# mLSTM products with queries on partitions and a ones column, head norm summed along rows, attention transposes one slot later

## What is computed

```python
num = einsum('bhcjs,bhcsd->bhcjd', P, v) + inter_w[..., None] * einsum('bhcde,bhcje->bhcjd', C_prev, q)
den = sum(P, axis=-1) + inter_w * einsum('bhce,bhcje->bhcj', n_prev, q)
h = num / maximum(abs(den), exp(-m_j))[..., None]
...
h = h_fw + h_bw
h = h * rsqrt(mean(h * h, axis=-1, keepdims=True) + EPS) * norm_g
y = sigmoid(o_pre) * h
```

## Time and profile before

| | us |
|---|---|
| median of 3 runs | 2229.85 (2228.08 to 2233.18) |
| the profiled execution, its own time | 2229.88 |
| its span, first to last instruction | 2228.1 |
| mean granted TensorE clock | 0.988 |
| first slot of cross attention to the first merge unit | 63.2 to 429.8 |

### The profile page before, as it was taken

The page is one execution under the profiler, slowest core; times in us unless marked ns, Lnnn a source line. Parts: engine busy times, 40 slices in busy tenths (PEclk is TensorE's granted clock), DMA queues, the critical chain, the costliest instruction groups (busy, mean ns, idle before and its releaser), DMA issues.

```text
span 2228.1 us, 29871 instructions
## 1 busy us (share of the span) xinstructions
PE 2153.9 (97%) x9840; PEld 1733.5 (78%) x9840; DVE 1019.4 (46%) x1694; ACT 864.7 (39%) x1252; POOL 1203.1 (54%) x1601
## 2 busy tenths in 40 slices
PE   6989999799999999999999999999999989999999
PEld 5867666588888888888878888887777767888887
DVE  5466587633345544223444555213655545554400
ACT  5334323443343443332134443324455445344321
POOL 7533322677755556655455556656444426655653
PEclk9989999899999999999999999999999999999999
DMA  6213411133333233333322323332322203223332
GB/s 217 89 48 109 114 49 38 48 99 104 109 95 94 94 96 103 95 93 95 104 88 93 104 94 93 96 102 68 116 90 71 86 29 103 95 94 104 91 102 72
DMA packets 61480, 205.06 MB, mean 92 GB/s; under 512 B 6848, under 2 KB 6976, under 8 KB 61392
## 3 DMA queue, kind: packets, MB, share of 16 engines
q1 hardware_dynamic: 61200, 203.65, 29.6%
q10 hardware_dynamic: 192, 0.30, 0.1%
HBM read 201.52 MB, written 2.39 MB: 92 GB/s over the span
## 4 chain that ended last, share of the span: by engine, by line
PE 87%; DVE 6%; ACT 2%; POOL 2%; DVEq 1%; issue 1%; DMA 1%; ACTq 0%; SPq 0%
PE bank L1424 27%; PE bank L1426 26%; PE bank L1425 26%; POOL WL L425 1%; PE bank L1632 1%; PE bank L1658 1%; PE bank L1644 1%; PE bank L1695 1%; PE bank L1697 1%; PE bank L1696 1%; PE bank L1465 1%; PE bank L1676 1%; DMA RAW<-in_w_att 0%; POOL YL L476 0%; PE bank L1561 0%
## 5 line engine op out<-in xcount | busy, mean ns | idle before, releaser
L425 POOL TENSOR_TENSOR WL<-RAW,WH 128x256 fp32r<-128x256 f32 x1496 | 1157.2, 807 | 967.7 <-ACT WH L537 967.3
L1424 PE MATMUL bank<-XH,WH 128*128 128x512 f32 x1840 | 728.5, 396 | 2.9 <-DVE XQ L896 2.0
L1426 PE MATMUL bank<-XH,WL 128*128 128x512 f32 x1840 | 717.1, 390 | 0.0
L1425 PE MATMUL bank<-XL,WH 128*128 128x512 f32 x1840 | 716.9, 390 | 0.0
L537 ACT ACTIVATE WH<-RAW 128x1024 fp32r<-128x1024 f32 x374 | 392.1, 1051 | 250.1 <-PE bank L1426 224.7
L1424 PEld LDWEIGHTS bank<-XH,WH 128*128 128x128 f32 x1840 | 345.9, 188 | 86.6 <-issue 5.4
L1425 PEld LDWEIGHTS bank<-XL,WH 128*128 128x128 f32 x1840 | 346.0, 188 | 73.7 <-issue 3.1
L1426 PEld LDWEIGHTS bank<-XH,WL 128*128 128x128 f32 x1840 | 345.8, 188 | 72.9
L1424 PE MATMUL bank<-FH,WH 128*128 128x512 f32 x528 | 205.4, 389 | 0.0
L1425 PE MATMUL bank<-FL,WH 128*128 128x512 f32 x528 | 205.4, 389 | 0.0
L1426 PE MATMUL bank<-FH,WL 128*128 128x512 f32 x528 | 205.4, 389 | 0.0
(11 more groups left out here) (277 smaller groups left out, 2441.6 us busy)
## 6 DMA issues: line engine op xcount, KB each, us to landing
RAW<-in_w_up SPq DMA_DIRECT2D x132, 512.0 KB, 3.5
RAW<-in_w_att SPq DMA_DIRECT2D x47, 512.0 KB, 3.6
RAW<-in_w_down SPq DMA_DIRECT2D x48, 448.0 KB, 3.3
RAW<-in_w_fa SPq DMA_DIRECT2D x32, 512.0 KB, 3.5
RAW<-in_w_down SPq DMA_DIRECT2D x24, 512.0 KB, 3.5
RAW<-in_w_ain SPq DMA_DIRECT2D x24, 512.0 KB, 3.5
RAW<-in_w_mrg SPq DMA_DIRECT2D x18, 512.0 KB, 3.6
RAW<-in_w_mrg SPq DMA_DIRECT2D x22, 256.0 KB, 2.7
```

What stands on the lines that cost most here:

```text
L425: last = nc.gpsimd.tensor_tensor(WL[:, s, w], RAW[:, s, w], WH[:, s, w].bitcast(F32), ALU.subtract)
L1424: mm(dst[:, 0:width], WH[:, s, w], a, start=start and k == 0, stop=False)
L1425: mm(dst[:, 0:width], WH[:, s, w], b, start=False, stop=False)
L1426: last = mm(dst[:, 0:width], WL[:, s, w], a, start=False, stop=stop and k == kc - 1)
```

## The change

1. mLSTM products: the decayed scores of a block of 128 queries are now the weights and the values the moving operand, `V` with a 129th column of ones beside it. A product gives numerator and denominator, queries on partitions. Five products of 129 columns a step take the place of four of up to 512. They fill three banks (`HBANK`).
2. The denominators are now 8 columns for a head; thresholds come transposed (`THR`, a new extra `thr`, four small transposes). `head_out` scales and adds in 128-column pieces. The norm is a row sum on ACT (`Square` with a sum), its scale is applied on ACT, and PE then turns the head back (`ht`, four transposes, one slot before where `hn` stood).
3. The exponents move from DVE to ACT (`Relu` with a bias, before `Exp`), with two buffers in turn. `UE` holds two rows a head instead of four: 6 row loads after the wait instead of 12, and one write of gates instead of two.
4. Attention: transposes of step g - 1 come in slot g and its products in slot g + 1, scaling likewise one slot later; buffers are halved in turn. The last attention slot transposes two steps.
5. The gain of the norm is applied where `YH` and `YL` of the mLSTM are formed.

```diff
+def lagging(st, lag):
+    if st and st in SIDX:
+        g = SIDX[st]
+        return tuple(STEPS[n] for n in (range(g - lag, g - lag + 1) if st != LAST_STEP else range(g - lag, g + 1))
+                     if n >= 0)
+    return ()
...
-    _ex = [("hn", _st[1] - 1)] if 3 in finishing(_st) else []
+    _ex = [("ht", _st[1] - 1)] if 2 in finishing(_st) else []
...
+    if _t == GATE_T + 5:
+        _ex.append(("tr", "thr", 0))
...
-                    for g in range(2):
-                        for d in range(2):
-                            row = gates_d[g, 32 * d + h, :]
-                            sp.dma_start(UE[:, UE_AT[h], 2 * g + d, :], row.partition_broadcast(P)).then_inc(ue_in, 16)
+                    for d in range(2):
+                        row = gates_d[0, 32 * d + h, :]
+                        sp.dma_start(UE[:, h, d, :], row.partition_broadcast(P)).then_inc(ue_in, 16)
...
             if st and st[0] == "ml":
-                act.wait_ge(e_arg, m + 1)
-                A_(SX[:, 0, P * s:S], SX[:, 0, P * s:S], ACT.Exp, scale=-1.0)
-                A_(SX[:, 1, 0:P * (s + 1)], SX[:, 1, 0:P * (s + 1)], ACT.Exp, scale=-1.0).then_inc(e_ready, 1)
...
+                    act.wait_ge(ms_read, m - 1)
+                for d in range(2):
+                    w = slice(P * s, S) if d == 0 else slice(0, P * (s + 1))
+                    A_(SXM[m % 2][:, d, w], UE[:, h, d, w], ACT.Relu, bias=UT[:, s, 32 * d + h:32 * d + h + 1])
+                act.drain()
+                for d in range(2):
+                    w = slice(P * s, S) if d == 0 else slice(0, P * (s + 1))
+                    e = SXM[m % 2][:, d, w]
+                    last = A_(e, e, ACT.Exp, scale=-1.0)
+                last.then_inc(e_ready, 1)
...
-                if 2 in finishing(st):
-                    act.wait_ge(h_ready, h + 1)
-                    A_(SQ[:], FI[:, 0, :], ACT.Square).then_inc(h_sq, 1)
+            if 1 in finishing(st):
+                act.preload_act_table_set(LN_EXP)
+                act.wait_ge(h_ready, h + 1)
+                for q in range(TB):
+                    A_(SQ[:, q * P:(q + 1) * P], HQ[:, q, :], ACT.Square, accum_out=HS[:, q:q + 1])
...
+                A_(HS[:], HS[:], ACT.Ln, scale=1.0 / P, bias=EPSC[:, 0:1])
...
+                A_(HS[:], HS[:], ACT.Exp, scale=-0.5)
...
+                for q in range(TB):
+                    last = A_(HQ[:, q, :], HQ[:, q, :], ACT.Copy, scale=HS[:, q:q + 1])
+                last.then_inc(h_rs, 1)
...
+        def head_out(h):
+            dve.wait_ge(mpv_done, 4 * h + 4)
+            for n, sl in ((0, slice(0, 3)), (1, slice(3, 6)), (2, slice(6, 8))):
+                den = HBANK[n][:, :, P]
+                thr = THR[:, 0:3, 32 * n + h] if n < 2 else THR[:, 3, h:64:32]
+                v.scalar_tensor_tensor(out=ND[:, sl], in0=den, scalar=-1.0, in1=thr, op0=ALU.mult, op1=ALU.max)
...
+            v.reciprocal(ND[:], ND[:])
+            for q in range(TB):
...
+                v.tensor_scalar(HQ[:, q, :], HBANK[b][:, n, 0:P], ND[:, c:c + 1], None, ALU.mult)
+            for q in range(TB):
...
+                last = v.scalar_tensor_tensor(out=HQ[:, q, :], in0=HBANK[b][:, n, 0:P], scalar=ND[:, c:c + 1],
+                                              in1=HQ[:, q, :], op0=ALU.mult, op1=ALU.add)
+            last.then_inc(nd_free, 1)
...
-            mm(bank[4][:, P * s:S], V[:, h % 2, s, :], fw, start=s == 0, stop=s == 3)
-            mm(bank[5][:, P * s:S], ONES[:], fw, start=s == 0, stop=s == 3)
-            mm(bank[6][:, 0:w], V[:, h % 2, s, :], bw, start=s == 0, stop=s == 3)
-            mm(bank[7][:, 0:w], ONES[:], bw, start=s == 0, stop=s == 3).then_inc(mpv_done, 1)
+            for d in range(2):
+                for q in range(s, TB) if d == 0 else range(s + 1):
+                    b, n = h_place(d, q)
+                    last = mm(HBANK[b][:, n, :], (PT, PB)[d][:, m % 2, P * q:P * (q + 1)], V[:, h % 2, s, :],
+                              start=first, stop=final)
+            last.then_inc(mpv_done, 1)
...
-            if before and before[0] in ("xa", "na"):
-                products(before)
+            for ts in lagging(st, 2):
+                if ts not in STEPS[-2:]:
+                    products(ts)
...
-            if st and st[0] in ("xa", "na"):
+            for ts in lagging(st, 1):
+                g = SIDX[ts]
                 for j in range(2):
                     pe.wait_ge(p_ready, 2 * g + j + 1)
```

More of the change, by code:

```diff
@@ L81, in finishing @@
         return ()
[L82 removed]
+    return (st[2],) if st[0] == "ml" else ((0, 1), (2,), (), ())[st[2]]
 UNITS = [u for u, _ in SLOTS if u is not None]
@@ L109 @@
             VEV[_e[1:]] = len(VEV)
-            if _e[1] != "nav64":
+            if _e[1] not in ("nav64", "thr"):
                 VSRC[_e[1:]] = len(VSRC)
@@ L292, in col, with turn_of, half_of, h_place @@
         return PAR[rows, bass.ds(COL[name] + n, 1)]
+    def turn_of(g, j):
+        return slice(2 * (g % 2) + j, 2 * (g % 2) + j + 1)
+    def half_of(t, g, j):
+        return t[:, j, M * (g % 2):M * (g % 2) + M]
+    HBANK = [bank[4][:, 0:3 * (P + 1)].rearrange("p (q e) -> p q e", e=P + 1),
+             bank[5][:, 0:3 * (P + 1)].rearrange("p (q e) -> p q e", e=P + 1),
+             bank[6][:, 0:2 * (P + 1)].rearrange("p (q e) -> p q e", e=P + 1)]
+    def h_place(d, q):
+        return (d, q) if q < 3 else (2, d)
+    def h_den(d, q):
+        return 3 * d + q if q < 3 else 6 + d
     def blk(t, n):
@@ L634, in _ @@
                     A_(TA[:], TC[:], ACT.Tanh, scale=0.5).then_inc(y_arg, 1)
-            if 3 in finishing(st):
-                act.preload_act_table_set(LN_EXP)
-                act.wait_ge(h_sum, st[1])
-                A_(TD[:], TD[:], ACT.Ln, scale=1.0 / P, bias=EPSC[:, 0:1])
-                act.drain()
-                A_(TD[:], TD[:], ACT.Exp, scale=-0.5).then_inc(h_rs, 1)
             if t == GATE_T + 1:
@@ L1010, in _ @@
                 v.tensor_tensor(PT[:, m % 2, dg], PT[:, m % 2, dg], LO[:], ALU.mult)
[L1011 to L1037 removed]
+                v.tensor_tensor(PB[:, m % 2, dg], PB[:, m % 2, dg], UP[:], ALU.mult).then_inc(mp_ready, 1)
+            if 0 in finishing(st):
+                head_out(st[1] - 1)
             if un:
@@ L1111, in _ @@
                 b = LB[LEV[e] % 2]
-                if e[0] == "hn":
-                    v.tensor_copy(TD[:], b[:]).then_inc(lin_free, 1)
-                    dve.drain().then_inc(h_sum, 1)
+                if e[0] == "ht":
+                    v.scalar_tensor_tensor(out=Y[:, 8 + e[1], :], in0=SO[:, e[1] % 2, :], scalar=1.0, in1=b[:],
+                                           op0=ALU.add, op1=ALU.mult).then_inc(lin_free, 1)
+                    dve.drain().then_inc(y_done, 1)
                     continue
@@ L1464, in products @@
                         w = VN[:, p % 2, KEY0[s] // 64 + 2 * k, 64 * j:64 * j + 64]
-                    last = mm(dst, w, PT[:, j, k * P:(k + 1) * P], start=k == 0, stop=k == MB - 1)
+                    last = mm(dst, w, half_of(PT, g, j)[:, k * P:(k + 1) * P], start=k == 0, stop=k == MB - 1)
                 last.then_inc(pv_done, 1)
@@ L1516, in _ @@
                     .then_inc(ms_full, 1)
-            if before and before[0] in ("xa", "na"):
-                products(before)
+            for ts in lagging(st, 2):
+                if ts not in STEPS[-2:]:
+                    products(ts)
+            if before == LAST_STEP:
+                for ts in STEPS[-2:]:
+                    products(ts)
             if before and before[0] == "ml":
@@ L1538, in _ @@
                 pe.wait_ge(lin_free, o + 1)
-                if e[0] == "hn":
-                    pe.wait_ge(h_sq, e[1] + 1)
-                    last = mm(LB[o % 2][:], ONES[:], SQ[:], start=True, stop=True)
-                elif e[1] == "gate":
-                    pe.wait_ge(v_src, VSRC[e[1:]] + 1)
-                    for k in range(TB):
-                        last = nc.tensor.transpose(LB[o % 2][:, 64 * k:64 * k + 64], GT[:, 3, P * k:P * (k + 1)],
+                if e[0] == "ht":
+                    pe.wait_ge(h_rs, e[1] + 1)
+                    for k in range(TB):
+                        last = nc.tensor.transpose(LB[o % 2][:, P * k:P * (k + 1)], HQ[:, k, :], IDN[:])
+                elif e[1] in ("gate", "thr"):
+                    if e[1] == "gate":
+                        pe.wait_ge(v_src, VSRC[e[1:]] + 1)
+                    else:
+                        pe.wait_ge(gate_act, 2)
+                    row = GT[:, 3, :] if e[1] == "gate" else GU[:, 1, :]
+                    for k in range(TB):
+                        last = nc.tensor.transpose(LB[o % 2][:, 64 * k:64 * k + 64], row[:, P * k:P * (k + 1)],
                                                    IDN[0:64, 0:64])
```

210 lines of the change are left out of this document (95 added, 115 removed).

## The result

| | before | changed |
|---|---|---|
| median of the runs | 2231.01 us (4 runs, 2228.08 to 2233.18) | 2192.23 us (4 runs, 2191.09 to 2196.18) |
| profiled execution, its span | 2229.88, 2228.1 | 2196.18, 2194.5 |
| PE busy, granted clock of the whole | 2153.9, as in the earlier trace rows | 2125.9, 0.991 |

The ratio is 0.983, with an interval of 0.9818 to 0.9842: 38.8 us less where the forecast had 41.5 (2188, range 2178 to 2202).

A forecast was written before the change was run, and what follows sets the result against it. PE, busy 97% of the span, was taken to bound the kernel. Terms -21.8 - 1.3 + 0.4 - 3.2 - 5.5 - 3.8 - 0.7 + 4.2 - 9.8 summed to -41.5, giving 2188 us, range 2178 to 2202.

The forecast's parts named there:

- Products, -21.8: mLSTM on PE: 80 products of 129 columns at 0.22 us, 17.8 in all, replace 39.6 us; gain 21.8.
- Rival D: mLSTM products: weight loads stand in the open, 30 us worse at 2218, or partly, 2206; 6%.
- Norm and linear bank, -1.3 and -3.2: Head norm: four transposes replace a 512-column product, gain 1.3; slot s = 3: wait on an unread linear bank goes, 3.2.
- Bank freeing and its clock, -5.5: mLSTM: PE's 3.9 us wait for freed banks goes, and 1.6 of low clock behind it.
- done before PE has ended the slot's unit: mLSTM `head_out`: its DVE operations take 3.4 us, so PE no longer waits for the banks.
- Head 0, -3.8: First mLSTM head: fewer row loads let the weight land earlier; PE's wait, 2.3, and slow columns, 1.5, go.
- ACT's order, +4.2: mLSTM: ACT's chain with the norm ahead of a `Tanh` makes PE wait; cost 4.2, 1.9 each in heads 1 and 2.
- the forecast for the mLSTM: From the first mLSTM scores to the start of the last slots: 32.1 us less.
- Attention, 0: Attention: lag takes `Exp` out of the path, but it was hidden; gain 0, bounds 3 gained and 2 lost.
- Last slots, -9.8: Last slots to the first merge unit: 33.9 us becomes 24 through earlier bank freeing and norm; gain 9.8.
- what was to be seen: Profile after: among other signs, no PE wait on bank freeing, and `YL` about 4 us after the last slots begin.
- Rival B: mLSTM: ACT binds harder, 4 to 5 us a head for heads 1 and 2, plus low clock; 2198; 18%.

The follow-up runs named there:

- twice: The changed kernel with each of the 80 mLSTM products issued two times, weight load included: 2205.22 us, ratio 0.9894 to the kernel before.
- rows_halved: The changed kernel with each row load for `UE` issued as two of 256 columns: 2194.13 us, ratio 0.9845 to the kernel before.
- rows_one_dma: The kernel before the change with the four rows of a head loaded by one DMA: 2232.12 us, ratio 1.0002.
- last_slots: The changed kernel with ACT's last norm, PE's turn of that head, DVE's `YL` and POOL's later subtractions reordered in the last slots: 2188.38 us, ratio 0.9814.
- control: The changed kernel run again without an edit, in the first series of experiments: 2196.36 us, ratio 0.9847 to the kernel before.
- turn_late: The changed kernel with ACT's norm of head 3 behind the first last-slot `Tanh` and PE's turn after the first branch unit: 2196.41 us, ratio 0.9846.
- lag_only: The kernel before the change with only the attention part of the change: 2226.39 us, ratio 0.9976.

## Why the prediction was right, and where it was not

The sign, the engine and the size were right: 38.8 and 33.7 us in two series, forecast 41.5, both times inside the range. Two terms were wrong, by 4.7 and by 6.1 us with opposite signs, and smaller misses in the mLSTM cancel in part as well. That the sum is better than its parts is luck.

- **Products, -21.8: right.** 0.21 from start to start (16 x 1.03 = 16.5 us where I had 17.8), 0.22 as a marginal price (twice). Rival D, and with it the rule of the Trainium skill, "TensorE: Matmul & The Clock Gate", The mechanism, that would leave the loads in the open, is excluded for this form: twice issues each of the 80 products again with its loads, and M is accounted for with none of them showing.
- **Norm and linear bank, -1.3 and -3.2: right as far as the view shows.** `ht` is four transposes, 0.44; no wait at L1597 in slot s = 3 (0.3 is left, in attention). Not tried singly.
- **Bank freeing and its clock, -5.5: 1.8 too much.** The clock is 1.00 through the mLSTM, and the 3.9 on `SS` are gone. But "done before PE has ended the slot's unit" failed: each of three heads has a wait of 0.38 us and a slot that is 0.6 longer.
- **Head 0, -3.8: right in size, wrong in half of its reason.** The wait of 2.28 us and the slow columns behind it are gone; the 0.4 that is left there is counted in the next point. "With 6 loads SP is free some 5 us earlier" doesn't matter; "half the bytes" does (rows_halved, rows_one_dma).
- **ACT's order, +4.2: the mechanism right, the size 1.15 short.** The waits are 0.25, 1.64, 0.29 and 1.66 where I had 0.5 and 0.8 to 1.4, twice; the slots are longer by 0.5 and 1.9 in each of heads 1 and 2, and by 0.4 in head 0, as forecast, though the view lists no wait there: 5.35 in all. What was missing is that a wait costs more than its listed length. The long ones stand ahead of the products of steps (1, 2) and (2, 2), one step later than the forecast named. Together with the 1.8 above, and less the 1.3 that the products are better, this makes 1.65 of the 1.9 us that are missing between the forecast for the mLSTM and its 30.2.
- **Attention, 0: wrong.** In the kernel before, the lag gains 4.7 (3.3 to 7.1), beyond the 3 that I gave as its bound; in the changed kernel no run tells it from the spread. The step that failed is "Only where ACT was late (one slot, 0.5 us) does something go": I weighed the length of the waits alone, and it did stay the same, 8.3 to 8.1. Their number I left out, 11 to 7, about 1 us; where the rest comes from, the clock or something else, is open.
- **Last slots, -9.8: wrong, 3.7.** "24 us" was 30.2. The step that failed is "the norm long done, DVE's two operations and the first `YL`, 2.5": these were 0.7 + 4.59 + 0.7 and more, because POOL, of which I had only asked when it would be ready, held up DVE's sum while its row ran. And I had put ACT's norm beside the branch units instead of ahead of `mg5`'s reading. Ordered otherwise the distance is what I had forecast: 24.3 in last_slots, counted from 0.9 us earlier, so 23.4.

Of what was to be seen, two lines failed: there are waits on bank freeing, and `YL` started 4.8 us after the last slots began, not 4. Rival B was nearest among the rest: two waits of 1.6, but at full clock.

## What to carry to other kernels

A wait of the bounding engine cost its listed length and about a quarter microsecond here, and one too short to be listed cost 0.4; compare the lengths of whole slots, or double the work behind the wait and see how little is added, since the work fills it. When an operation is moved to an idle engine, write down what stands behind it in that engine's order: here ACT's exponents, and in one slot of four the ten small operations and two table loads of the norm ahead of the `Tanh`, cost PE 5.35 us in the mLSTM, and forming the exponentials one step early, with the buffers that existed, took most of it back. At the end of a stage ask of each engine not only when it is ready but what it keeps from its neighbour.

## What the runs showed of the hardware

- A DVE operation with two operands in SBUF, 0.69 us with GpSimd idle, took 1.5 to 6.0 us here beside a row of GpSimd subtractions without gaps; with one operand in a bank it took 0.69 beside the same row. In five of eight profiles of the changed kernel and its like it ended 0.55 us after the last of the row, with 4 to 5.5 us of the row left at its start; in three it slipped in, and in the kernel before too (0.95), and beside the next row it took 0.83 and 0.69. The Trainium skill, "SBUF — State Buffer", Who interferes with whom, has the mechanism: "A DVE instruction with two SBUF inputs contends with a GpSimd instruction that reads SBUF". That it can wait for the rest of a row and not for the one instruction in progress is what these traces add.
- Where DVE got in, GpSimd's row was longer: its 20 subtractions took 13.8 us where DVE was shut out, 15.65 in the control.
- A weight load of 512 KB behind 3 MB of row loads lands at the same time whether these are 3 issues or 12 (ACT starts on it at 260.10 and 260.01, after 3.76 us of waiting both times), though SP issues it at 241.80 or at 249.96.
- ACT's two table loads last 1.28 us each, and the next operation starts at once (373.10 + 1.28, 374.39), in the last slots as in the earlier trace rows.
- With nearly equal waits the granted clock of a stretch of 10 us between 130 and 160 us was anywhere between 0.72 (turn_late, 150 to 160) and 1.00 (lag_only, all three) from one profile to the next, and the mLSTM started between 231.7 and 237.5 us. A difference of under 5 us between two single profiles has to be read from a stretch, not from their ends.
